# Value products of two attentions: head by head, or by pairs of heads on two column tiles

## The reference

```
z = einsum('bqhd,bkhd->bhqk', q_blk, k) * scale
log_beta = log_sigmoid(z)
log_1mb = where(mask, log_sigmoid(-z), 0.0)
suffix = cumsum(log_1mb, reverse=True) - log_1mb
att = where(mask, exp(log_beta + suffix), 0.0)
out = einsum('bhqk,bkhd->bqhd', att, v)
```

```
s = einsum('bhqd,bhkd->bhqk', q_blk, kh) + fq_blk[..., None] - F[:, :, None, :]
s = where(k_pos <= q_pos, s, -inf)
p = softmax(s)
out = einsum('bhqk,bhkd->bhqd', p, vh)
```

## Time and profile before

| | us |
|---|---|
| median of 3 runs (1363.07 to 1365.45) | 1365.0 |
| the profiled execution, its own time | 1362.18 |
| its span | 1360.4 |
| PE busy in the span | 1326.9 |
| block 1's attention, first scores of head 2 to `sum_squares(N_ATT)` | 145.97 to 211.98 |
| block 2's attention, first scores of head 2 to `branch_part(3)` | 873.56 to 920.94 |

### The profile page before, as it was taken

How to read it: one execution, slowest core, us unless ns; L and a number is a source line. 1 busy time by engine, 2 the same in 40 slices (tenths; PEclk the granted TensorE clock), 3 DMA queues, 4 the chain that set the end, 5 groups by cost and what they waited for, 6 DMA issues and landing times.

```text
span 1360.4 us, 15770 instructions
## 1 busy us (share of the span) xinstructions
PE 1326.9 (98%) x6278; PEld 1074.5 (79%) x6278; DVE 777.6 (57%) x885; ACT 510.3 (38%) x575; POOL 108.3 (8%) x100
## 2 busy tenths in 40 slices
PE   7999999899999999997999999999999999999997
PEld 5777667688888889995888888767888888888886
DVE  7797654933333357876436433556676767664222
ACT  6463653412222235454212322464343334332122
POOL 4003010300000011224000001000310000000000
PEclk9999999999999999999999999999999999999999
DMA  5322001132222369541342222201322223232221
GB/s 167 123 93 93 32 1 62 62 123 93 92 92 92 123 150 270 105 101 49 125 155 93 93 93 93 93 1 43 112 93 92 93 92 112 73 123 93 75 96 62
DMA packets 103348, 130.35 MB, mean 96 GB/s; under 512 B 3338, under 2 KB 80378, under 8 KB 103170
## 3 DMA queue, kind: packets, MB, share of 16 engines
q1 hardware_dynamic: 97282, 115.99, 25.7%
q0 software_dynamic: 6000, 13.65, 5.1%
q10 hardware_dynamic: 16, 0.00, 0.0%
HBM read 127.52 MB, written 2.11 MB: 95 GB/s over the span
## 4 chain that ended last, share of the span: by engine, by line
PE 88%; DVE 5%; issue 3%; POOL 2%; ACT 2%; DMA 0%; ACTq 0%; SPq 0%; DVEq 0%; POOLq 0%
PE psum L1519 25%; PE psum L1521 25%; PE psum L1520 25%; PE psum L1637 3%; DVE w_lo L940 2%; PE psum L1664 2%; PE psum L1652 1%; POOL tmp L563 1%; PE psum L1789 1%; ACT w_hi L622 1%; PE psum L1790 1%; PE psum L1791 1%; PE psum L1847 1%; DVE act_lo L949 1%; DVE xT L1151 1%
## 5 line engine op out<-in xcount | busy, mean ns | idle before, releaser
L1519 PE MATMUL psum<-act_hi,w_hi 128*128 128x512 f32 x1224 | 485.7, 397 | 13.9 <-DVE act_lo L949 6.6
L1521 PE MATMUL psum<-act_hi,w_lo 128*128 128x512 f32 x1224 | 481.3, 393 | 0.0
L1520 PE MATMUL psum<-act_lo,w_hi 128*128 128x512 f32 x1224 | 477.6, 390 | 0.0
L622 ACT ACTIVATE w_hi<-raw 128x2048 fp32r<-128x2048 f32 (+1 forms) x102 | 192.4, 1887 | 590.6 <-PE psum L1521 579.6
L940 DVE TENSOR_TENSOR w_lo<-raw,w_hi 128x2048 fp32r<-128x2048 f32 (+1 forms) x102 | 233.7, 2291 | 126.8 <-ACT w_hi L622 126.8
L1519 PEld LDWEIGHTS psum<-act_hi,w_hi 128*128 128x128 f32 x1224 | 230.4, 188 | 70.3 <-issue 13.2
L1520 PEld LDWEIGHTS psum<-act_lo,w_hi 128*128 128x128 f32 x1224 | 230.3, 188 | 52.4 <-issue 1.4
L1521 PEld LDWEIGHTS psum<-act_hi,w_lo 128*128 128x128 f32 x1224 | 230.3, 188 | 51.3
L1789 PE MATMUL psum<-part_hi,w_hi 128*128 128x256 f32 x308 | 86.7, 282 | 1.3 <-DVE w_lo L940 1.3
L1790 PE MATMUL psum<-part_lo,w_hi 128*128 128x256 f32 x308 | 86.1, 279 | 0.0
L1791 PE MATMUL psum<-part_hi,w_lo 128*128 128x256 f32 x308 | 86.0, 279 | 0.0
(11 more groups left out here) (260 smaller groups left out, 1508.8 us busy)
## 6 DMA issues: line engine op xcount, KB each, us to landing
raw<-in_w_in SPq DMA_DIRECT2D x30, 1024.0 KB, 5.1
raw<-in_w_ffn_in SPq DMA_DIRECT2D x22, 1024.0 KB, 5.0
raw<-in_w_up SPq DMA_DIRECT2D x22, 1024.0 KB, 5.0
raw<-in_w_down SPq DMA_DIRECT2D x10, 1024.0 KB, 4.9
x_buf<-in_w_ffn_out POOLq DMA_DIRECT2D x6, 1024.0 KB, 10.1
raw<-in_w_out SPq DMA_DIRECT2D x4, 1024.0 KB, 4.9
raw<-in_w_o SPq DMA_DIRECT2D x4, 1024.0 KB, 5.1
x_buf<-in_w_ffn_out POOLq DMA_DIRECT2D x3, 768.0 KB, 10.6
```

What stands on the lines that cost most here:

```text
L622: A(w_hi[:, s % 2, 0:n], home(s, n), ACT.Copy).then_inc(w_hi_ready, 1)
L1519: mm(dst, stationary[0], moving[0], start=first, stop=False)
L1520: mm(dst, stationary[0], moving[1], start=False, stop=False)
L1521: return mm(dst, stationary[1], moving[0], start=False, stop=last)
```

## The change

The value products of two heads are written as one piece: for each key block first head h's matmul and then head h+1's, so that neighbouring matmuls go to the two column tiles in turn. The pair's products stand where the second head's stood: after `suffix(h)` or `turn_probs(h)` for h = 2, 4, 6. The last pair of block 1 comes after the slab `S_OUT_LRU`, and the last pair of block 2 after `branch_part(2)`. The weights get more room: those of head 2 go to `spare` (laid over chunks 5 to 7 of `act_hi`), those of head 6 to `lx` in block 1 and to `neg_f` in block 2. The early parts move: (0,0) after head 3, (0,2) after head 4, both of the second after head 5.

```diff
-EARLY, EARLY_HEAD = 2, 3
+EARLY = 2
-def early_part(h):
-    return ((h - EARLY_HEAD) // 2, 2 * ((h - EARLY_HEAD) % 2)) if EARLY_HEAD <= h < EARLY_HEAD + 2 * EARLY else None
+EARLY_PARTS = {3: [(0, 0)], 4: [(0, 2)], 5: [(1, 0), (1, 2)]}
+EARLY_ADDED = {5: 0, 7: 1}
...
+        spare = nc.alloc_sbuf_tensor_at("spare", [P, CAUSAL], F32, offset=act_base + 4 * 5 * TOKENS)
+        att_of = [att[:, 0], att[:, 1], spare, att[:, 1], att[:, 0], att[:, 1], flat(lx[:, 0:3]), att[:, 1]]
+        probs_of = [probs_T[:, 0], probs_T[:, 1], spare, probs_T[:, 1], probs_T[:, 0], probs_T[:, 1], flat(neg_f[:, 0:3]),
+                    probs_T[:, 1]]
...
             def weights(h):
                 act.wait_ge(suffix_done, h + 1)
-                if h >= 2:
-                    act.wait_ge(pv_done, h - 1)
+                if h == 2:
+                    act.wait_ge(slab_done, S_V + 2)
+                if h >= 3 and h != 6:
+                    act.wait_ge(pv_done, h - 1 if h % 2 else 2)
+                if h == 6:
+                    act.wait_ge(act_lo_ready, C_LRU + WC)
...
             def values(h, weights, v_rows, bank):
-                p = HD * (h % 2)
                 for kb in range(TB):
                     n = TOKENS - kb * P
-                    ins = mm(psum[p:p + HD, bank, kb * P:TOKENS], v_rows[:, kb, h * HD:(h + 1) * HD],
-                             weights[:, h % 2, KEY_AT[kb]:KEY_AT[kb] + n], start=kb == 0, stop=kb == TB - 1,
-                             skip_group_check=True)
+                    for e in range(2):
+                        ins = mm(psum[e * HD:(e + 1) * HD, bank, kb * P:TOKENS], v_rows[:, kb, (h + e) * HD:(h + e + 1) * HD],
+                                 weights[h + e][:, KEY_AT[kb]:KEY_AT[kb] + n], start=kb == 0, stop=kb == TB - 1,
+                                 skip_group_check=True)
                 return ins
...
             for h in range(1, HEADS):
                 if h + 1 < HEADS:
                     scores_kq(h + 1)
-                if h == 1:
-                    values_kq(h - 1)
                 suffix(h)
-                if h > 1:
-                    values_kq(h - 1)
-                if early_part(h):
+                if h % 2 == 0:
+                    values_kq(h - 2)
+                for m, k0 in EARLY_PARTS.get(h, ()):
...
-            pe.wait_ge(att_ready, 2 * HEADS)
-            values_kq(HEADS - 1)
+            pe.wait_ge(att_ready, 2 * (HEADS - 1))
             slab_b(S_OUT_LRU, act_part, q=C_LRU, order=range(EARLY, 4))
+            values_kq(HEADS - 2)
             pe.wait_ge(src_ready, C_ATT + WC)
             sum_squares(N_ATT, 0)
...
                 if h == HEADS - 1:
-                    values_qk(h - 1)
+                    pe.wait_ge(pt_ready, 2 * h)
                     branch_part(1)
                 turn_probs(h)
...
-                if h < HEADS - 1:
-                    values_qk(h - 1)
+                if h % 2 == 0:
+                    values_qk(h - 2)
             branch_part(2)
-            values_qk(HEADS - 1)
+            values_qk(HEADS - 2)
             branch_part(3)
```

More of the change, by code:

```diff
@@ L333, in two_blocks, with flat @@
         act_scope.close()
+        def flat(x):
+            return x.rearrange("p a n -> p (a n)")[:, 0:CAUSAL]
+        spare = nc.alloc_sbuf_tensor_at("spare", [P, CAUSAL], F32, offset=act_base + 4 * 5 * TOKENS)
+        att_of = [att[:, 0], att[:, 1], spare, att[:, 1], att[:, 0], att[:, 1], flat(lx[:, 0:3]), att[:, 1]]
+        probs_of = [probs_T[:, 0], probs_T[:, 1], spare, probs_T[:, 1], probs_T[:, 0], probs_T[:, 1], flat(neg_f[:, 0:3]),
+                    probs_T[:, 1]]
         xnat = sb("xnat", [P, TB, D], F32, act_scope)
@@ L706, in weights @@
                 act.wait_ge(suffix_done, h + 1)
-                if h >= 2:
-                    act.wait_ge(pv_done, h - 1)
+                if h == 2:
[4 more added lines that the diff above has]
+                    act.wait_ge(act_lo_ready, C_LRU + WC)
                 b = head_bank(h)
                 for n0, n1 in ((0, TOKENS), (TOKENS, CAUSAL)):
-                    A(att[:, h % 2, n0:n1], psum[:, b:b + 3].rearrange("p b n -> p (b n)")[:, n0:n1], ACT.Exp).then_inc(att_ready, 1)
+                    A(att_of[h][:, n0:n1], psum[:, b:b + 3].rearrange("p b n -> p (b n)")[:, n0:n1], ACT.Exp).then_inc(att_ready, 1)
             log_part(0)
@@ L835, in _ @@
                 act.wait_ge(pt_done, h + 1)
-                if h >= 2:
-                    act.wait_ge(pv2_done, h - 1)
+                if h == 2:
+                    act.wait_ge(slab_done, S_OA2)
+                if h >= 3 and h != 6:
+                    act.wait_ge(pv2_done, h - 1 if h % 2 else 2)
+                if h == 6:
+                    act.wait_ge(s_max, 3 * TB)
                 b = head_bank(h)
                 for n0, n1 in ((0, TOKENS), (TOKENS, CAUSAL)):
-                    A(probs_T[:, h % 2, n0:n1], psum[:, b:b + 3].rearrange("p b n -> p (b n)")[:, n0:n1], ACT.Copy).then_inc(pt_ready, 1)
+                    A(probs_of[h][:, n0:n1], psum[:, b:b + 3].rearrange("p b n -> p (b n)")[:, n0:n1], ACT.Copy).then_inc(pt_ready, 1)
                 if h >= 2 and h % 2 == 0:
@@ L1116, in _ @@
                     split_act(C_LRU + c, act_hi[:, c], act_lo[:, c], lx[:, c], col("norm_lru_out", c))
-                if h > EARLY_HEAD and early_part(h - 1) and early_part(h - 1)[1]:
-                    m = early_part(h - 1)[0]
+                if h in EARLY_ADDED:
+                    m = EARLY_ADDED[h]
                     dve.wait_ge(early_done, m + 1)
@@ L1678, in values_kq @@
             def values_kq(h):
-                pe.wait_ge(att_ready, 2 * h + 2)
-                if h >= 2 and h % 2 == 0:
+                pe.wait_ge(att_ready, 2 * h + 4)
+                if h >= 2:
                     pe.wait_ge(src_ready, C_ATT + h // 2)
-                values(h, att, v, 0).then_inc(pv_done, 1)
+                values(h, att_of, v, 0).then_inc(pv_done, 2)
             pe.wait_ge(gate_read, WC)
@@ L1708, in _ @@
                     scores_kq(h + 1)
-                if h == 1:
-                    values_kq(h - 1)
                 suffix(h)
-                if h > 1:
-                    values_kq(h - 1)
-                if early_part(h):
-                    m, k0 = early_part(h)
-                    if h == EARLY_HEAD:
+                if h % 2 == 0:
+                    values_kq(h - 2)
+                for m, k0 in EARLY_PARTS.get(h, ()):
+                    if m == 0 and k0 == 0:
                         wait_w(S_OUT_LRU)
@@ L1863, in values_qk @@
             def values_qk(h):
-                pe.wait_ge(pt_ready, 2 * h + 2)
-                if h >= 4 and h % 2 == 0:
+                pe.wait_ge(pt_ready, 2 * h + 4)
+                if h >= 4:
                     pe.wait_ge(act_lo_ready, C_O2 + h // 2 - 1)
-                values(h, probs_T, v2, pair_bank(h // 2)).then_inc(pv2_done, 1)
+                values(h, probs_of, v2, pair_bank(h // 2)).then_inc(pv2_done, 2)
             s = S_OA2 - 1
```

## The result

| | before | with the change |
|---|---|---|
| median | 1365.22 us (1361.85 to 1366.6, 14 runs) | 1359.11 us (1357.98 to 1363.18, 14 runs) |
| ratio | | 0.9959, 95% interval 0.995 to 0.9968 |
| profiled execution, own time | 1362.18 | 1359.25 |
| its span | 1360.4 | 1357.5 |
| PE busy | 1326.9 | 1315.9 |

The change is faster by 0.41%, 5.6 us (4.4 to 6.8); the ratio is taken over all runs, and the two medians alone stand 6.1 us apart. The forecast was 9.0 us and 1356.0: the direction was right, more than a third of the gain did not come, and the median lies at the upper edge of the range.

What follows compares the result with a forecast made beforehand. PE, busy 98% of the span, was taken as the bound. Removing 16.4 + 1.2 us and laying bare 8.3 of waits left 9.3, taken as 9.0: 1356.0 us against the median 1365.0, range 1352.5 to 1359.5.

Steps and rivals of the forecast that it cites:

- eight pairs: Value blocks of both attentions: pairs written in turn take 2.35 us each, 18.8 for 35.2, so 16.4 us less.
- six changes of form fewer, slow first products: Both attentions: fewer switches between 64-column and full products save 1.2 us; slower first products after waits lose a few tenths.
- (a): Block 1, scores of head 3: PE waits 1.75 us instead of 0.69 for head 1's first Exp on ACT, 1.1 lost.
- (b): Block 1, scores of head 5: ACT needs 4.6 us, PE has 4.4 of work, 0.2 lost.
- (c): Block 1, suffix of head 7: `soft_lo` ready at 7.6 us, PE there at 7.1, 0.5 lost.
- (d): End of block 1: `sum_squares` waits 2.9 us for DVE's copy, ACT's square and POOL's sum; the largest single wait.
- (e): Block 2, scores of heads 3, 5 and 7: each waits 0.75 us for ACT's first copy, 2.2 lost.
- (f): Block 2, `branch_part(1)`: PE waits 1.4 us for DVE's `act_lo` of heads 4 and 5.
- clock behind (d): After the `sum_squares` wait: forecast kept full clock; the rival, chance 0.15, had half speed costing 1.5 to 1.7 us, 1357.6.
- The overlap: Value products of two heads on different tiles stream together at full rate, as read from 0.7 us of before's 3.86.
- Strict order between the tiles: Rival, chance 0.05: in each pair the second head trails by a 512-column record, 2.7 us a pair, 3.0 less gain, 1359.

Runs made afterwards that it cites:

- e3: The changed kernel with block 2's attention given back its old order and weights, so the change in block 1 alone; 1360.46 us, ratio 0.9971.
- e5: The changed kernel with the second head's four products written behind the first's within each pair, not in turn; 1369.19 us, ratio 1.0037.
- e8: The changed kernel with each pair's heads alternating by two key blocks instead of one; 1359.6 us, ratio 0.9958.
- e1: The changed kernel with twelve extra products, read by nobody, in the wait before `sum_squares`; 1357.49 us, ratio 0.9948.
- e7: The changed kernel with five extra products, read by nobody, behind block 1's last pair, leaving about half the wait before `sum_squares`; 1357.06 us, ratio 0.9937.
- e2: The changed kernel with block 1's last pair moved between the slab's two column groups, so twelve dense products stand behind it; 1354.47 us, ratio 0.9922.
- e4: The changed kernel with block 1's attention given back its old order and weights, so the change in block 2 alone; 1360.82 us, ratio 0.9961.
- r_before_again: The kernel before the change, unaltered, measured and profiled a second time; 1363.9 us, ratio 0.9994.

## Why the forecast was wrong in its size

Point by point, forecast against the profile after.

| step | forecast | measured |
|---|---|---|
| eight pairs | 8 x 2.35, 16.4 removed | 8 x 2.30, 16.8 removed |
| six changes of form fewer, slow first products | 0.9 less (1.2 - 0.3) | about nothing together |
| (a) scores of head 3 | 1.1 (a wait of 1.75 for 0.69) | 1.66 for 0.69: 0.97 |
| (b) scores of head 5 | 0.2 | 0.21 |
| (c) suffix of head 7 | 0.5 | 0.37 idle, and some 0.4 within the suffix |
| (d) `sum_squares` | 2.9 | 2.89 |
| (e) scores in block 2 | 2.2 | 0.78 + 0.69 + 0.69 = 2.16 |
| (f) `branch_part(1)` | 1.4 | 1.51 |
| block 1 | 3.8 less | 3.87 less |
| block 2 | 5.2 less | 4.46 less |
| clock behind (d) | full | low for 3.4 us: 1.7 more |

**The step that failed is the clock behind (d).** The forecast named it as a rival, with the right place, length and price (1.5 to 1.7), and then set it at 0.15, on one comparison: 2.9 us is shorter than the 3.4 us of the earlier trace rows. One pause behind which the clock falls says nothing of shorter ones. From 10 us on, the profile of before had pauses of up to 1.7 us with the clock staying and one of 3.4 with it falling, and nothing between. So the rows left it open, with a chance near a half, and half of the price belonged into the sum. The clock measured 1.71 us. All five profiled executions with this pause of 2.9 us (the change twice, e3, e5, e8) have the low stretch behind it; none of those without it has one there, and e1 and e7 remove it by work that serves nothing else. This cause is shown.

**The second term that was off is the 1.2 for changes of form, counted as if only they made a product slow.** In before, scores after a value block start with 0.91 us for two records and scores behind an early part with 0.81: 0.1 for the change of form. But in the profile after, scores behind a wait have the same 0.91 (153.94, 169.07), with no change of form before them. Where a value block was taken away, a wait mostly took its place and the 0.1 stayed. It shows in block 2: 4 x 2.30 for 17.6 makes 8.4 less, the waits (e) and (f) 3.7 more, 4.7 in all, and 4.46 is what came. In block 1 something was saved: scores of head 2 take 2.62 us for 2.71, the suffixes of heads 3 and 5 2.83 for 2.92 and 2.81 for 2.90, and two early parts in a row 2.76 for twice 1.50. Together the two blocks give 16.8 - 8.1 = 8.7 by pairs and idle time and 8.3 by their lengths; the rest, 0.4, is the size of what the suffix of head 7 lost beside its idle time. Savings of form and slow first products thus about cancel, where the forecast had 0.9 less. No run takes the two apart.

So the forecast's 9.0 becomes 6.6 by these steps: 1.7 less for the clock, 0.9 less for form and first products, 0.4 less for what the suffix of head 7 lost beside its idle time (0.26 of it the wait for `soft_lo`), 0.4 more for the pairs and 0.2 more since the idle time is 8.1 and not 8.3.

**The waits held, but for half of (c).** Their sum was put at 8.3 and their idle time is 8.1, none off by more than 0.13. In (c) the forecast had PE wait for `soft_lo` only. PE first waits for `soft`, which the forecast did not check, and then for `soft_lo` within the suffix, so that the real cost is near 0.8 and not 0.5. Each wait was made of a chain of durations from before's rows, which the change does not alter. The check of (d) against after: values end, DVE copies at 206.00, ACT squares at 206.72, POOL adds at 207.43 and `sum_squares` starts at 208.84.

```profile
206.00 0.69 DVE L1112 COPY qT<-psum 128x512 f32<-128x512 f32 x1 [7.27 <-PE psum L1652]
```

```profile
206.72 0.63 ACT L635 ACTIVATE tmp<-qT 128x512 f32<-128x512 f32 x1 [6.11 <-DVE qT L1112]
```

```profile
207.43 1.27 POOL L570 TENSOR_TENSOR tmp<-tmp 128x512 f32<-128x512 f32 x1 [6.06 <-ACT tmp L635]
```

**The overlap was right for a reason that was half wrong.** The forecast read before's 3.86 us as head 7 waiting for its weights until 203.91. e5 shows the same 3.86 and the same 1.56 with weights long ready. What it built on, that the two tiles stream at full rate side by side, is true; that the late start was the weights' fault is not. Had the change written the heads in a row, this reading would have promised 2.3 us a pair and got 3.86.

**The rule on order.** The Trainium skill, "TensorE: Matmul & The Clock Gate", Part 3, "What overlaps and what doesn't", has matmuls start and end in program order. With neighbours in turn the rows neither refute nor need it: starts are 0.01 us apart, in the order of the program, and the second head does not trail by a record (the rival of 2.7 us a pair). In e5 the trace disagrees: the six loads in 0.62 us are those of both heads mixed, so the second head's first record (161.71) starts while three of the first head's (161.93, 162.14, 162.25) have not yet started. In e8 it disagrees too: the second head's first record starts at 159.26, ahead of the first head's second at 159.73.

**The rival with the nearest time was wrong.** Strict order between the tiles gave 1359, within 0.1 of the median, and its mechanism is absent. A time alone would have confirmed it.

Stays open: 6.6 us by the traces against 5.6 and, the second time, 6.1 (4.4 to 8.0) by the medians. Both intervals hold 6.6; the rate of the dense products (below), which no kernel here controls, is enough to blur more than that.

## What to carry to other kernels

Here the 64-column products of two heads, in plain float32, ran together for their whole length only where the program handed them to PE nearly alternately (by one or by two products); moving them next to each other without that made things worse. Taking PE work away lays waits bare, and most of their sizes can be worked out to 0.1 us from the chains of before; but the wait of 2.9 us also had a price behind it, half of 3.4 us at the lower clock, so break such a wait up or put a slab's last group behind the work it waits for (e2 won some 4 us by that alone). Judge a change of a few us by the lengths of the stretches it touches, not by two profiled spans.

## What the runs showed of the hardware that was not expected

**Two rates of the same products at the same clock.** With a granted clock of 1.00 and PE never idle, dense 512-column products start either 0.2289 or 0.2333 us apart, over stretches of a hundred us and more. Which it is differs between executions of one program (before: 657 and 645 records in 150 us) and at different places: between 300 and 450 us e8 has the slower one, e7 the faster, in code that is the same:

```profile
300.00:450.00 150.00, 150.00 (x645) 1.00 0.29 97
```

```profile
300.00:450.00 150.00, 150.00 (x657) 1.00 0.29 96
```

That e8's profiled execution took 1363.49 against a median of 1359.6 is mostly this. The cause was not tried.

**When the clock falls.** 2.9 us of pause before `sum_squares`: it fell five times of five. The 1.54 of e7: not. The 2.24 us ahead of 604 us: in e1, e2 and e4, but not in e3 nor in r_before_again. And in e5 not even a pause of 3.4 us, at a place where the other executions have a low stretch:

```profile
250.31:253.69 3.38, 0.00 (x0) 1.00 0.00 0
253.70:257.10 3.40, 3.40 (x15) 1.00 0.61 212
```

And in block 2 e5 has a low stretch with no long pause ahead of it. The longest idle times of PE in the 11 us before it are 0.78 (here) and 0.48, around ten transposes:

```profile
883.01 1.76 PE L1859 MATMUL psum<-k,q_odd 128*128 128x512 f32 x2 [0.78 <-ACT tmp L855]
```

```profile
880.00:883.30 3.30, 1.92 (x12) 1.00 0.72 245
883.31:886.71 3.40, 3.40 (x9) 0.50 0.00 0
```

The changed kernel has the same two idle times there and keeps the clock. So the length of the pause is not all that decides; how PE's work before it comes in was not separated out. A low stretch costs less where other engines are late anyway: the changed kernel has 6.8 us of it from 246.76, before 3.4 from 249.24. The lead of 1.43 us at the restart drops to 0.35 at 256 us and is 1.28 again from 263 on, so the 3.4 us more of low clock cost 0.15 us.
